# Second mixer: index scores rectified in PSUM, rounds moved between the low parts, differential output scaled late, weights of the second tile ahead

## The chip, the cores and the metric

One NeuronCore of a Trainium2 chip runs the whole program in one launch. The metric is the device time of an execution in microseconds (us); the value of a kernel is the median of its runs. All times in this document are us unless marked otherwise.

## The reference, cut to what matters

256 tokens of width 1024 in float32 pass through two blocks of two layers each. The change touches only the mixer of the second block (`hybrid_layer`), which is run twice (layer 0 and layer 1):

```python
h = rms_norm_2(x, attn_norm); proj = h @ w_in            # 1024 x 5444
aq, ak, av, iq, ik, iw, bq, bk, bv, gates = split_cols(proj)
# heads are normed and rotated; then, for path A (8 heads of 64, in pairs):
dots  = einsum(iq, ik) * 64**-0.5                        # 4 index heads
score = sum_h iw[h] * relu(dots[h]);  score[not causal] = -inf
top 64 keys of each query by score                       # k_sel = 256 // 4
ya = softmax(q k * 64**-0.5 over those keys) @ v
# path B (4 differential pairs): p0, p1 are two causal softmaxes
yb = (p0 - lam * p1) @ v;  yb = rms_norm_2(yb, b_subln) * (1 - lam_init)
x = x + (g_a * (ya @ w_up_a) + g_b * (yb @ w_up_b)) @ w_out
x = x + swiglu of rms_norm_2(x)                          # FFN, hidden 2816
```

The first block (FFN, another mixer, FFN, twice, then a norm) runs ahead of it, and its last norm is folded into the first norm of layer 0 here.

## The kernel before, in words

**Products.** Every float32 product with weights is made of three matmuls of the fast float32 form: high part by high part, high by low, low by high (`three`). A weight unit is 128 x 2048 elements (`raw`, four slots). It is loaded by a DMA from the SyncE queue, ScalarE writes its high part (`split` in the scalar block, to `w_hi`, line 717), VectorE subtracts that from the unit to get the low part (`split` in the vector block, `w_lo`, line 1222), and TensorE waits for `units_split`. A slot is used again four units later. `win_split(n, j)` is the split of unit j of tile n.

**Projection.** The 5444 columns are 11 tiles (`WIN2`), each of two units and 16 steps; a step is three matmuls of 128 x 128 by up to 512 columns. `full_k` runs a tile: its steps are numbered 0 to 15 (8 j + 4 i + c: unit j, token half i), and after each step it calls a function of the tile (`beside_bk`, `beside_aq`, ...) which may put other work on TensorE between the steps. Tile 2 (bk), 3 (aq), 4 (bv), 5 (ak), 6 (av), 7 to 10 (gates). Two PSUM banks take a tile; ScalarE evacuates both halves (`evac_half`), for the gates VectorE does (`gate`). GpSimd rotates the heads of a tile (`rotate2`) and signals `rot_ready`.

**What lies beside.** `turn(k)` transposes rotated heads by the identity, and `item(k)` copies them out of PSUM (even on ScalarE, odd on VectorE). `index_scores(h0)` puts the raw scores of two index heads into banks 4 and 5; ScalarE rectifies and scales them into `xn` (`index_relu`, signal `idx_relu`); VectorE adds them up with their weights (`index_score`, signal `idx_used`). `best(1)` is a round that finds the 8 largest scores of each token and marks them (`V.max`, `V.match_replace`, lines 1741 and 1744); eight rounds give 64. Then the marks are made a mask, which `masked(k)` adds for pairs 4 to 7.

**A pair** (0 to 3 differential, 4 to 7 sparse) passes through `pair_qk` (TensorE, banks 4 and 5), `masked` (VectorE), `exps` (ScalarE), `probs` (VectorE), `pair_turn` (TensorE, banks 6 and 7), `probs_turned` (ScalarE and, from pair 4 on, VectorE too), `diff_pv` or `sparse_pv` (TensorE), and, for a differential pair, `diff_out` (ScalarE, bank 2 to `xn`). After the norm of path B, TensorE turns it into banks 6 and 7, `diff_hi` and `diff_lo` split it, and `pair_turn(7)` waits for `diff_lo`, since it uses the same banks.

**Order.** Each engine's order is written out by hand in its block: a call that waits holds everything after it on that engine. There is no planner.

Of the kernel before, what the change touches and what calls it, by code (L numbers as in the profile page):

```python
# [15 lines left out]
ALU = mybir.AluOpType  # L16
ACT = mybir.ActivationFunctionType
# [5 lines left out]
P = 128  # L23
# [6 lines left out]
DH = 64  # L30
# [25 lines left out]
P2_WIN = 0  # L56
# [52 lines left out]
def build(nc, I, out):  # L109
    L = DEPTH  # L110
    with ExitStack() as ctx:
# [295 lines left out]

        relu = xn[:, :, 0:384]
# [299 lines left out]
        def _(act):  # L708
# [281 lines left out]
            for l in range(L):  # L990
# [4 lines left out]
                if l == 0:  # L995
# [8 lines left out]
                    square(6, 0, junk, 2)  # L1004
                    square_scaled(0)
                    stage(B, GAIN_ATTN, PARTS[2:], first=2)
                    split(st, 2)
# [52 lines left out]
                def index_relu(h):  # L1060

                    act.wait_ge(idx_done, l * 4 + h + 1)
                    if h >= 2:
                        act.wait_ge(idx_used, l * 4 + h - 1)
                    nc.scalar.activation(relu[:, h % 2, :], ps[:, 4 + h % 2, 0:384], ACT.Relu, scale=DH ** -0.5)\
                        .then_inc(idx_relu, 1)
# [19 lines left out]
                def diff_out(k):  # L1086

                    act.wait_ge(pair_out, J + (k + 1))
                    nc.scalar.activation(xn[:, :, 512 + P * k:512 + P * k + P],
                                         ps[:, 2, 0:2 * P].rearrange("p (i d) -> p i d", i=2), ACT.Copy)\  # L1090
                        .then_inc(diff_evac, 1)
# [21 lines left out]
                split(st, 3)  # L1113
# [29 lines left out]
                item(4)  # L1143
                head_roots(3)
                win_split(6, 0)
                act.wait_ge(lam_sums, l + 1)
                nc.scalar.activation(lam[:, 0:2], lam[:, 0:2], ACT.Exp).then_inc(lam_exp, 1)
                evac_half(4, 0)
# [38 lines left out]
                exps(7)  # L1187
                split(st, P2_UP + 1)
                diff_hi()
# [22 lines left out]
        def _(dve):  # L1212
# [453 lines left out]
            for l in range(L):  # L1666
# [3 lines left out]
                if l == 0:  # L1670
                    stage(B, GAIN_ATTN, PARTS[2:], first=2)
                    split(st, 2)
                    two_norms(N)
                    split(st, 3)
# [52 lines left out]
                def index_score(h):  # L1727

                    dve.wait_ge(idx_relu, l * 4 + h + 1)
                    for i, (c, n) in enumerate(((0, P), (P, 2 * P))):  # L1730
                        V.scalar_tensor_tensor(score[:, c:c + n], relu[:, h % 2, c:c + n], iw[:, i, h:h + 1],  # L1731
# [28 lines left out]
                def probs(k):  # L1760
# [3 lines left out]
                    V.drain()  # L1764
                    for i, (c, n) in enumerate(((0, P), (P, 2 * P))):
                        p0, p1 = (pair_p[:, k % 2, e, c:c + n] for e in range(2))
                        f0, f1 = (pair_factor[:, k % 2, e, i:i + 1] for e in range(2))
                        if k < 4:
                            V.tensor_scalar(p1, p1, f1, lam[:, 2:3], ALU.mult, ALU.mult)
# [3 lines left out]
                    if k < 4:  # L1773
                        V.drain()
                        for i, (c, n) in enumerate(((0, P), (P, 2 * P))):
                            p0, p1 = (pair_p[:, k % 2, e, c:c + n] for e in range(2))
# [972 lines left out]
```

## Time and profile before

| | |
|---|---|
| median of 3 runs | 1790.29 us (1788.45 to 1790.33) |
| the profiled execution | 1788.07 us, span of its instructions 1786.4 us |
| granted TensorE clock | 1.00 in every slice |
| busy: TensorE, VectorE, ScalarE, GpSimd | 99%, 69%, 55%, 13% of the span |
| second mixer, layer 0 | about 1020.9 to 1190 us |
| second mixer, layer 1 | about 1400 to 1570 us |

A timeline row is: start from the beginning of the span, duration, engine, line of the kernel, operation, output<-inputs by the program's names, shapes, count; in brackets idle time ahead of it and what ended it. Matmuls overlap: the next starts long before the drawn end of the one before. A `windows` row is: stretch, its length, then busy us and number of instructions of TensorE's matmuls, its weight loads, VectorE, ScalarE and GpSimd, then the granted clock, the DMA share and GB/s. Names: PE is TensorE, DVE VectorE, ACT ScalarE, POOL GpSimd.

### The profile page before, as it was taken

How to read it: one execution, taken by the hardware profiler on the slowest of the kernel's cores; microseconds unless marked ns; L12 is line 12 of the kernel's file. 1: busy time of each engine (PE TensorE's matmuls, PEld its weight loads, DVE VectorE, ACT ScalarE, POOL GpSimd, SP SyncE). 2: the span in 40 equal slices, each digit the busy share in tenths (PEclk: the TensorE clock that was granted, in tenths of full speed). 3: DMA queues.
4: the chain of work that ended last, by engine and by line, in shares of the span. 5: the costliest groups of instructions: out<-in, count | busy, mean ns of one | idle time of the engine just before them, and what ended most of it. 6: DMA issues, size and time to landing. Idle time of an engine off the chain costs nothing.

```text
span 1786.4 us, 25450 instructions
## 1 busy us (share of the span) xinstructions
PE 1773.3 (99%) x9448; PEld 1479.0 (83%) x9448; DVE 1231.7 (69%) x1753; ACT 988.0 (55%) x1333; POOL 226.2 (13%) x255
## 2 busy tenths in 40 slices
PE   9999999999999999999999999999999999999999
PEld 8888877888888888877888877778888877788887
DVE  6775667677557755767776489976775599867763
ACT  6554586565445554666555476555554466645551
POOL 0000131000000000320000096200001383100000
PEclk9999999999999999999999999999999999999999
DMA  8756472555546564544665563535656544545651
GB/s 266 221 195 203 138 211 73 188 188 188 212 145 195 194 224 143 190 119 143 195 197 198 166 212 124 181 128 182 201 195 207 168 162 143 188 159 173 192 202 75
DMA packets 221517, 316.26 MB, mean 177 GB/s; under 512 B 14168, under 2 KB 162288, under 8 KB 221168
## 3 DMA queue, kind: packets, MB, share of 16 engines
q1 hardware_dynamic: 221392, 315.02, 54.1%
q8 instruction: 57, 0.93, 0.2%
q14 instruction: 36, 0.29, 0.0%
q10 hardware_dynamic: 32, 0.01, 0.0%
HBM read 313.94 MB, written 1.05 MB: 176 GB/s over the span
## 4 chain that ended last, share of the span: by engine, by line
PE 84%; DVE 9%; DVEq 3%; ACT 2%; issue 1%; ACTq 0%; POOL 0%; POOLq 0%
PE ps L2091 25%; PE ps L1955 14%; PE ps L1957 13%; PE ps L1956 13%; PE ps L2092 13%; DVE w_lo L1222 3%; PE ps L1965 1%; ACT w_hi L717 1%; PE ps L2206 1%; PE ps L2179 1%; DVEq L1706 1%; PE ps L2194 1%; DVEq L1742 1%; DVE score L1731 1%; DVE att L1755 1%
## 5 line engine op out<-in xcount | busy, mean ns | idle before, releaser
L1222 DVE TENSOR_TENSOR w_lo<-raw,w_hi 128x2048 fp32r<-128x2048 f32 (+2 forms) x296 | 674.5, 2301 | 200.9 <-ACT w_hi L717 199.2
L2091 PE MATMUL ps<-aT,w_hi 128*128 128x512 f32 x1920 | 667.9, 392 | 0.0
L717 ACT ACTIVATE w_hi<-raw 128x2048 fp32r<-128x2048 f32 (+2 forms) x296 | 551.5, 1891 | 158.9 <-PE ps L1957 155.7
L2092 PE MATMUL ps<-aT,w_lo 128*128 128x256 f32 x1920 | 537.7, 280 | 0.0
L2091 PEld LDWEIGHTS ps<-aT,w_hi 128*128 128x128 f32 x1920 | 359.2, 187 | 79.8 <-issue 0.3
L2092 PEld LDWEIGHTS ps<-aT,w_lo 128*128 128x128 f32 x1920 | 362.9, 189 | 0.2
L1955 PE MATMUL ps<-w_hi,aT 128*128 128x512 f32 (+2 forms) x768 | 309.3, 403 | 4.3 <-DVE w_lo L1222 2.8
L1957 PE MATMUL ps<-w_hi,aT 128*128 128x512 f32 (+2 forms) x768 | 295.1, 384 | 0.0
L1956 PE MATMUL ps<-w_lo,aT 128*128 128x512 f32 (+2 forms) x768 | 294.2, 383 | 0.0
L1955 PE MATMUL ps<-w_hi,gT_hi 128*128 128x512 f32 x528 | 206.0, 390 | 0.0
L1957 PE MATMUL ps<-w_hi,gT_lo 128*128 128x512 f32 x528 | 205.6, 389 | 0.0
L1956 PE MATMUL ps<-w_lo,gT_hi 128*128 128x512 f32 x528 | 205.5, 389 | 0.0
L1955 PEld LDWEIGHTS ps<-w_hi,aT 128*128 128x128 f32 x768 | 144.3, 188 | 46.1 <-issue 16.6
L1957 PEld LDWEIGHTS ps<-w_hi,aT 128*128 128x128 f32 x768 | 144.1, 188 | 29.2
L1956 PEld LDWEIGHTS ps<-w_lo,aT 128*128 128x128 f32 x768 | 144.6, 188 | 22.9
L766 ACT ACTIVATE att<-ps 128x512 f32<-128x512 f32 x60 | 35.9, 599 | 162.6 <-PE ps L2092 162.5
L1957 PEld LDWEIGHTS ps<-w_hi,gT_lo 128*128 128x128 f32 x528 | 99.1, 188 | 20.8
L1955 PEld LDWEIGHTS ps<-w_hi,gT_hi 128*128 128x128 f32 x528 | 99.1, 188 | 20.5
L1956 PEld LDWEIGHTS ps<-w_lo,gT_hi 128*128 128x128 f32 x528 | 99.1, 188 | 20.2
L1313 DVE TENSOR_TENSOR att<-ps,att 128x512 f32<-128x512 f32 x60 | 41.5, 692 | 78.6 <-ACT att L771 78.6
L768 ACT ACTIVATE att<-att 128x512 f32<-128x512 f32 x60 | 37.9, 632 | 103.8 <-DVE att L1311 103.8
L618 POOL COPY tt<-proj 128x512 f32<-128x512 f32 x4 | 4.1, 1052 | 634.3 <-DVE proj L1453 634.3
(289 smaller groups left out, 1704.0 us busy)
## 6 DMA issues: line engine op xcount, KB each, us to landing
raw<-in_w_in SPq DMA_DIRECT2D x120, 512.0 KB, 4.6
raw<-in_w_ffn_down SPq DMA_DIRECT2D x88, 512.0 KB, 4.4
raw<-in_w_ffn_in SPq DMA_DIRECT2D x88, 512.0 KB, 5.0
raw<-in_w_ffn_gate SPq DMA_DIRECT2D x86, 512.0 KB, 4.1
raw<-in_w_ffn_up SPq DMA_DIRECT2D x86, 512.0 KB, 5.1
raw<-in_w_ffn_out SPq DMA_DIRECT2D x44, 512.0 KB, 4.7
raw<-in_w_out SPq DMA_DIRECT2D x32, 512.0 KB, 4.7
raw<-in_w_ck SPq DMA_DIRECT2D x8, 512.0 KB, 3.9
```

The source lines that it names most:

```text
L717: nc.scalar.activation(dst, src, ACT.Copy).then_inc(units_hi, 1)
L766: nc.scalar.activation(sil[:, b % 2], ps[:, bg:bg + 2, SEQ:2 * SEQ], ACT.Copy).then_inc(gate_lo, 1)
L768: nc.scalar.activation(sil[:, b % 2], sil[:, b % 2], ACT.Silu).then_inc(silu_done, 1)
L1222: V.tensor_tensor(o, a, h, ALU.subtract).then_inc(units_split, 1)
L1313: V.tensor_tensor(gg[:, b % 2], ps[:, bu:bu + 2, 0:SEQ], gg[:, b % 2], ALU.add)
L1706: V.drain()
L1731: V.scalar_tensor_tensor(score[:, c:c + n], relu[:, h % 2, c:c + n], iw[:, i, h:h + 1], (causal if h == 0 else score)[:, c:c + n], ALU.mul ...
L1955: M(o, ah, wh, start=start, stop=False)
L1956: M(o, ah, wl, start=False, stop=False)
L1957: return M(o, al, wh, start=False, stop=stop)
L2091: M(o, wh, aT[:, :, k, :], start=k == 0, stop=False, skip_group_check=True)
L2092: r = M(o[:, 0], wl, aT_hi[:, k, :], start=False, stop=k == KC - 1, skip_group_check=True)
```

## The change

In the mixer of the second block:

- `index_relu` rectifies in place, in PSUM; `index_score` reads the bank. So `index_scores(2)` and `pair_qk(0)`, which write these banks again, wait for VectorE's `idx_used` where they waited for ScalarE's `idx_relu`, and ScalarE no longer waits for a free half of `relu`.
- The places on TensorE move: the first turn from after step 8 to after step 11 of tile bk, the first index scores from 14 to 15, the second ones from step 2 to step 8 of tile aq, the second turn from 9 to 11.
- For a differential pair VectorE forms lam x s0 / s1 (s the sums of the exponentials), adds p1 times this to the unscaled p0 in one operation for each half, and `diff_out` on ScalarE applies 1 / s0, in two operations.
- Rounds: before 1 after split(5, 0), 1 after probs(1), 2 after head_scales(4), 2 after masked(3), 2 after gate(7, 0). Now 1 ahead of split(5, 0), 1 behind it, 1 after head_sums(3), 1 ahead of probs(0), 1 ahead of masked(1), 1 after probs(1), 1 after head_scales(4), 1 after masked(3). The mask is made ahead of split 16 of the projection, and gate(7, 0) comes behind masked(4).
- ScalarE: item(4) comes behind evac_half(4, 0), head_roots(3) and the exponential of lam.
- `diff_hi` and `diff_lo` come ahead of the split of unit P2_UP + 1 (on VectorE gate(10, 0) too).
- Layer 0 only: units 2 and 3 (the second tile's weights) are split ahead of the squares of the folded norm and its roots.

```diff
-                    square_scaled(0)
-                    stage(B, GAIN_ATTN, PARTS[2:], first=2)
                     split(st, 2)
+                    stage(B, GAIN_ATTN, PARTS[2:], first=2)
+                    split(st, 3)
+                    square_scaled(0)
...
                     act.wait_ge(idx_done, l * 4 + h + 1)
-                    if h >= 2:
-                        act.wait_ge(idx_used, l * 4 + h - 1)
-                    nc.scalar.activation(relu[:, h % 2, :], ps[:, 4 + h % 2, 0:384], ACT.Relu, scale=DH ** -0.5)\
-                        .then_inc(idx_relu, 1)
+                    bank = ps[:, 4 + h % 2, 0:384]
+                    nc.scalar.activation(bank, bank, ACT.Relu, scale=DH ** -0.5).then_inc(idx_relu, 1)
...
-                    nc.scalar.activation(xn[:, :, 512 + P * k:512 + P * k + P],
-                                         ps[:, 2, 0:2 * P].rearrange("p (i d) -> p i d", i=2), ACT.Copy)\
-                        .then_inc(diff_evac, 1)
+                    for i in range(2):
+                        o = nc.scalar.activation(xn[:, i, 512 + P * k:512 + P * k + P], ps[:, 2, P * i:P * i + P],
+                                                 ACT.Copy, scale=pair_factor[:, k % 2, 0, i:i + 1])
+                    o.then_inc(diff_evac, 1)
...
-                item(4)
+                win_split(6, 0)
+                evac_half(4, 0)
                 head_roots(3)
-                win_split(6, 0)
                 act.wait_ge(lam_sums, l + 1)
                 nc.scalar.activation(lam[:, 0:2], lam[:, 0:2], ACT.Exp).then_inc(lam_exp, 1)
-                evac_half(4, 0)
+                item(4)
...
                 exps(7)
+                diff_hi()
                 split(st, P2_UP + 1)
-                diff_hi()
...
                     split(st, 2)
+                    split(st, 3)
                     two_norms(N)
-                    split(st, 3)
...
-                        V.scalar_tensor_tensor(score[:, c:c + n], relu[:, h % 2, c:c + n], iw[:, i, h:h + 1],
+                        V.scalar_tensor_tensor(score[:, c:c + n], ps[:, 4 + h % 2, c:c + n], iw[:, i, h:h + 1],
...
+                    if k < 4:
+                        f1 = pair_factor[:, k % 2, 1, :]
+                        V.scalar_tensor_tensor(f1, f1, lam[:, 2:3], pair_sums[:, k % 2, 0, :], ALU.mult, ALU.mult)
+                        V.drain()
...
-                            V.tensor_scalar(p1, p1, f1, lam[:, 2:3], ALU.mult, ALU.mult)
+                            o = V.scalar_tensor_tensor(p0, p1, f1, p0, ALU.mult, ALU.add)
...
-                    if k < 4:
-                        V.drain()
-                        for i, (c, n) in enumerate(((0, P), (P, 2 * P))):
-                            p0, p1 = (pair_p[:, k % 2, e, c:c + n] for e in range(2))
-                            o = V.scalar_tensor_tensor(p0, p0, pair_factor[:, k % 2, 0, i:i + 1], p1, ALU.mult, ALU.add)
...
                 item(3)
+                best(1)
                 win_split(5, 0)
                 best(1)
+                win_split(5, 1)
                 head_sums(3)
+                best(1)
                 item(5)
-                win_split(5, 1)
                 masked(0)
...
+                best(1)
                 probs(0)
                 win_split(6, 0)
+                best(1)
                 masked(1)
...
-                best(2)
+                best(1)
                 split(st, P2_WIN + 15)
                 masked(3)
-                best(2)
+                best(1)
                 probs(3)
                 item(9)
-                split(st, P2_WIN + 16)
-                dve.wait_ge(bias_loaded, (l + 1) * 16)
-                dve.wait_ge(rot_ready, l * 5 + (4 * L + 5))
-                gate(7, 0)
-                best(2)
...
+                split(st, P2_WIN + 16)
                 masked(4)
+                dve.wait_ge(bias_loaded, (l + 1) * 16)
+                dve.wait_ge(rot_ready, l * 5 + (4 * L + 5))
+                gate(7, 0)
                 split(st, P2_WIN + 17)
...
                 probs(7)
-                split(st, P2_UP + 1)
                 diff_lo()
                 gate(10, 0)
+                split(st, P2_UP + 1)
                 split(st, P2_UP + 2)
...
                 def beside_bk(at):
-                    if at == 8:
+                    if at == 11:
                         rotated(0)
                         turn((0, 1))
-                    if at == 14:
+                    if at == 15:
...
                 def beside_aq(at):
-                    if at == 2:
-                        pe.wait_ge(idx_relu, l * 4 + 2)
+                    if at == 8:
+                        pe.wait_ge(idx_used, l * 4 + 2)
                         index_scores(2)
-                    if at == 9:
+                    if at == 11:
...
-                        pe.wait_ge(idx_relu, l * 4 + 4)
+                        pe.wait_ge(idx_used, l * 4 + 4)
                         pair_qk(0)
```

## Rows read from the trace of the kernel before

**Rows 1.** The page, busy time of each engine.
```profile
PE 1773.3 (99%) x9448; PEld 1479.0 (83%) x9448; DVE 1231.7 (69%) x1753; ACT 988.0 (55%) x1333; POOL 226.2 (13%) x255
```

**Rows 2.** Busy time in the second mixer of layer 0 and of layer 1.
```profile
1020.90:1190.00 169.10, 165.16 (x840) 129.61 (x839) 143.87 (x257) 108.69 (x173) 84.88 (x73) 1.00 0.49 162
1400.00:1570.00 170.00, 166.83 (x849) 131.14 (x848) 143.62 (x259) 106.01 (x174) 77.06 (x53) 1.00 0.49 161
```

**Rows 3.** Timeline of TensorE, layer 0, third tile: start, duration, instruction.
```profile
1039.97 0.39 PE L1955 MATMUL ps<-w_hi,aT 128*128 128x512 f32 x1
...
1047.91 0.39 PE L1957 MATMUL ps<-w_hi,aT 128*128 128x512 f32 x1
```

**Rows 4.** Timeline of TensorE, layer 0: starts that are late, idle in brackets.
```profile
1029.22 0.31 PE L1957 MATMUL ps<-w_hi,aT 128*128 128x324 f32 x1
1029.94 0.50 PE L1955 MATMUL ps<-w_hi,aT 128*128 128x512 f32 x1 [0.41 <-DVE w_lo L1222]
...
1036.44 0.50 PE L1955 MATMUL ps<-w_hi,aT 128*128 128x512 f32 x1 [0.72 <-DVE w_lo L1222]
...
1083.89 0.50 PE L1955 MATMUL ps<-w_hi,aT 128*128 128x512 f32 x1 [0.29 <-ACT proj L1031]
...
1089.25 0.39 PE L1957 MATMUL ps<-w_hi,aT 128*128 128x512 f32 x1
1089.78 0.55 PE L2505 MATMUL ps<-ident,att 128*128 128x128 f32 x3
...
1131.28 0.50 PE L1955 MATMUL ps<-w_hi,aT 128*128 128x512 f32 x1 [0.86 <-DVE w_lo L1222]
...
1167.68 0.84 PE L2505 MATMUL ps<-ident,att 128*128 128x128 f32 x6 [0.88 <-DVE yb_lo L1796]
```

**Rows 5.** Timeline of TensorE, layer 0: first turn, index scores, first pair, last pair.
```profile
1048.13 0.66 PE L2137 MATMUL ps<-ident,proj 128*128 128x128 f32 x4
...
1056.88 0.93 PE L2477 MATMUL ps<-tt 64*128 64x128 f32 x8
...
1080.38 0.93 PE L2490 MATMUL ps<-tt 64*128 64x128 f32 x8
...
1171.24 0.87 PE L2532 MATMUL ps<-xn,proj 128*64 128x256 f32 x8
```

**Rows 6.** Timeline of VectorE, layer 0.
```profile
1052.40 3.19 DVE L1222 TENSOR_TENSOR w_lo<-raw,w_hi 128x2048 fp32r<-128x2048 f32 x1 [0.17 <-ACT w_hi L717]
...
1055.68 3.22 DVE L1222 TENSOR_TENSOR w_lo<-raw,w_hi 128x2048 fp32r<-128x2048 f32 x1
...
1060.73 2.11 DVE L1731 SCALAR_TENSOR_TENSOR score<-xn,iw,score 128x128 f32<-128x128 f32 x2
...
1079.61 0.68 DVE L1355 TENSOR_SCALAR tt<-ps 128x512 f32<-128x512 f32 x1
...
1083.38 0.41 DVE L1755 CUSTOM_DVE_ANT_0 att<-ps,causal 128x256 f32<-128x256 f32 x1
...
1095.65 0.67 DVE L1769 TENSOR_SCALAR att<-att,factor,lam 128x128 f32<-128x128 f32 x2
...
1115.20 0.61 DVE L1741 MAX8 m<-score 128x8 f32<-128x128 f32 x2
...
1116.71 0.62 DVE L1741 MAX8 m<-score 128x8 f32<-128x128 f32 x2
...
1128.93 2.29 DVE L1222 TENSOR_TENSOR w_lo<-raw,w_hi 128x2048 fp32r<-128x2048 f32 x1
...
1167.45 0.74 DVE L1703 SCALAR_TENSOR_TENSOR proj<-ps,rstd,proj 128x512 f32<-128x512 f32 x1
...
1170.50 0.55 DVE L1785 COPY xn<-ps 128x384 f32<-128x384 f32 x1
```

**Rows 7.** Timeline of GpSimd, layer 0, fourth rotation.
```profile
1081.04 3.35 POOL L656 TENSOR_TENSOR proj<-proj,rg 128x512 f32<-128x512 f32 x1
```

**Rows 8.** Timeline of ScalarE, layer 0, before the exponential of lam.
```profile
1081.76 1.28 ACT L1147 ACT_TABLE_LOAD   x1
```

More of the change, by code:

```diff
@@ L406, in build @@
         HEAD_NORMS = ((0, 1792, 64, 2), (1, 1860, 32, 3), (2, 2372, 48, 4), (3, 0, 0, 0), (5, 512, 16, 1))
-        relu = xn[:, :, 0:384]
         h1 = tt1[0:60, 14:16, :].rearrange("p a n -> p (a n)").rearrange("p (k n) -> p k n", k=2)
@@ L1004, in _ @@
                     square(6, 0, junk, 2)
+                    split(st, 2)
+                    stage(B, GAIN_ATTN, PARTS[2:], first=2)
+                    split(st, 3)
                     square_scaled(0)
-                    stage(B, GAIN_ATTN, PARTS[2:], first=2)
-                    split(st, 2)
                     square(6, 1, junk, 2)
@@ L1112, in _ @@
                 evac(0)
-                split(st, 3)
+                if l > 0:
+                    split(st, 3)
                 head_squares(0)
@@ L1672, in _ @@
                     split(st, 2)
+                    split(st, 3)
                     two_norms(N)
-                    split(st, 3)
                 else:
```

## The prediction

> **What bounds the kernel now.** I read the page first. TensorE (PE) is busy in 99% of a span of 1786.4 us [rows 1]. That share says little, since matmuls overlap: one of 512 columns is shown as 0.39 us long, but from the start at 1039.97 to that at 1047.91 there are 35 of them, so the pitch is 7.94 / 35 = 0.227 us [rows 3]. A step of a projection tile is three matmuls, 0.68 us. PE is the bound while its starts keep this pitch, and all that the change can win is the time by which a start is later. So the second view is PE's timeline through the second mixer, about 1021 to 1190 us for layer 0 and 1400 to 1570 for layer 1. VectorE (DVE) is busy for 143.9 of 169.1 us in the first stretch and 143.6 of 170.0 in the second, so its queue, not ScalarE's (108.7), is the one that can be late for PE [rows 2].
>
> I price a stall as the distance between two starts less the usual one. Where the view prints an idle time, it counts from the drawn end, so 0.39 - 0.227 = 0.16 is added. Layer 0 has, by [rows 4]: on w_lo at 1029.94, 0.72 behind a matmul of 324 columns at 1029.22 whose own pitch I estimate at 324 / 512 x 0.227 = 0.14, so 0.58; 0.72 + 0.16 = 0.88 on w_lo at 1036.44; 0.29 + 0.16 = 0.45 on ScalarE's evacuation at 1083.89; 0.86 + 0.16 = 1.02 on w_lo at 1131.28; 0.88 + 0.16 = 1.04 on yb_lo at 1167.68. Where a turn by identity follows a matmul without a wait, its distance is 1048.13 - 1047.91, the pitch; at 1089.78 it is 0.53, a stall of 0.30. Of such small stalls there are five in each layer, between 0.06 and 0.38, together about 1.1. Layer 1 repeats the pattern, except for the first two, which belong to layer 0's start. The whole prize is thus 1.46 + 2 x (0.45 + 1.02 + 1.04 + 1.1) = 8.7 us, 0.49% of the span. No edit can be worth more.
>
> **Layer 0's second tile (units 2 and 3).** The splits of both units now come on ScalarE before the squares of the final norm, and on DVE before two_norms. ScalarE can start unit 2 right behind the first square, and DVE's two splits (2.29 each where nothing else runs, as at 1128.93 [rows 6]) then follow the staging directly: both stalls, 0.58 + 0.88 = 1.46, should go. The price is that the norm, and with it the first tile's evacuation, is later by an estimated 1.5 to 2 us (one split more ahead of it). What depends on that is GpSimd's (POOL's) first rotation. PE used it at 1048.13 [rows 5]; that job moves three steps back (8 to 11), which gives 2.04 us. Taken as hidden; if the cover is gone, it costs up to 1.
>
> **Rectified scores in PSUM.** The index score read xn, iw and score from SBUF: 2.11 for a head's two operations (at 1060.73) [rows 6], four heads per layer. A DVE operation with two tensors in SBUF waits for a POOL operation that runs, and the other way round: w_lo at 1055.68 takes 3.22 in place of 2.29, and POOL's product at 1081.04 takes 3.35 [rows 6, 7]. An operation with one tensor in PSUM doesn't: the masked scores at 1083.38 take 0.41 while that product is in flight. The new score is of this kind; by this row I take 0.7 for a head (0.28 + 0.41 for its 128 and 256 columns; between 0.6 and 0.8), so DVE gains 1.4 a head, 5.6 a layer. The ScalarE part writes PSUM where it wrote SBUF, with the same 384 columns; I put it at no change.
>
> The Trainium skill (VectorE: DVE Perf Modes, section on the TRN2 errata) gives a fixed part of 120 cycles for a PSUM source and 58 for an SBUF one, which speaks against this edit: 65 ns for each of the 16 operations. The row of 0.41 for 256 columns agrees with the higher figure (0.39). By the page the gain would be 5.1 a layer where I take 5.6; PE's time would move by no more than that difference at one wait.
>
> But the edit adds a wait. PE may write banks 4 and 5 again only when DVE has read them: index_scores(2) and pair_qk(0) now wait for idx_used. PE's side: the old place is 1056.88 [rows 5], six steps earlier than the new one, so 1060.9. DVE's side: the first turn moves three steps back, to 1050.2, and with it the chain item(0), head squares, split (3,1), which began 4.27 behind the turn (1052.40 against 1048.13) [rows 5, 6]: now 1054.4. Then come two splits, 2.3 each free or 3.2 each beside POOL, and two heads of 0.7: 1060.4 to 1062.2. POOL rotates in all of this stretch, so I take 1061.8: **a new stall of 0.9 in each layer, bounds 0 and 1.4**. Behind it on PE's queue is everything.
>
> **Rounds moved ahead.** A round is 1.51 (1115.20 to 1116.71) [rows 6]. Eight remain. Before, one lay ahead of item(5); now three do, and split (5,1) too. DVE up to item(5): -5.6 (scores) + 3.0 (two rounds) + 2.3 to 3.2 (split) + 2.0 (the turn that starts the chain is later, and DVE waits for it) = 1.7 to 2.6 later than 1079.61 + 0.68 [rows 6]. That is 1082.0 to 1082.9. PE wants pair_qk(0), which waits for item(5), at 1080.32 + 0.9 = 1081.2 [rows 5]. ScalarE's item(4) now stands behind head_roots(3) and the exponential's table (1.28) [rows 8] and so comes about 2.4 behind head_sums(3), the same as DVE's round and item(5). POOL's third rotation meets three splits instead of two, which can hold turn((4, 5)) by the same amount. **New stall here: 1.3 in each layer, bounds 0 (no collisions) and 2.8 (each of three splits and a small operation waits 1.3 for POOL).** In return evac_half(4, 0) comes ahead of the roots and the table: 0.45 gone.
>
> What the early rounds buy lies at 1131.28: split(17) stood behind the last two rounds, the final mask and masked(4). With six rounds done before and masked(4) bound by pair_qk(4) alone, it ends some 3 us before it is wanted. 1.02 gone, and the following small stalls too: I take the 1.1 of them whole.
>
> **Differential output.** Two tensor_scalar for each of four pairs go (0.67 for both without POOL, at 1095.65) [rows 6], one tiny product and its drain come (about 0.2): 0.5 or more per pair off DVE, 2 a layer, most of it in stretches in which DVE then waits for PE. ScalarE gets a second operation of 128 columns, about 0.3, four times, beside idle time. Nothing on PE.
>
> **diff_hi and diff_lo ahead of P2_UP + 1.** The stall of 1.04 goes: diff_lo no longer waits behind a split of 2.3. But gate(10, 0) now stands ahead of both splits, and it can't begin before step 11 of the last tile has ended, 0.68 before the unstalled turn: 1167.68 - 1.04 - 0.68 = 1165.96, with the tail of the pipe 1166.1. Then gate 0.74, two splits 2.2 each, the copy of probs_turned(7) 0.55 (rows at 1167.45, 1128.93 and 1170.50) [rows 6]: 1171.8, and PE a little behind it. sparse_pv(7) needs this copy and ran at 1171.24 [rows 5]. PE thus gets there 0.7 later than now, not 1.0 earlier: **-0.7 in each layer**; bounds +1.0 (the copy is in time after all) and -1.2.
>
> **Sum.** Gains 1.46 + 2 x (0.45 + 1.02 + 1.1) = 6.6; new waits 2 x (0.9 + 1.3 + 0.7) = 5.8. Left: 0.8 us faster. The profiled execution took 1788.07 (span 1786.4 and 1.7 around it), 2.2 below the median of 1790.29; I subtract from the median: 1789.5.
>
> **Rivals.** (1) The new waits don't bite: if DVE's splits fall between POOL's operations, idx_used comes at 1060.4, item(5) before 1081, and only the tail is lost. 6.6 - 1.4 = 5.2 faster, 1785.1; with the tail won as well, 8.7, 1781.6. For it: DVE gains 5.6 a layer where it was never idle. Against it: the chain starts 2 us later and POOL is busy throughout. (2) Slower, by one mechanism: VectorE's queue ahead of item(5) and head_sums(3). Three rounds and both splits of tile 5 stand there, and if the splits each wait for POOL, pair_qk(0) stalls 2.8 and the index wait 1.4, in both layers: 2 x (1.4 + 2.8 + 0.7) - 6.6 = 3.2 slower, 1793.5; with the tail at its bound of -1.2 it is 4.2, 1794.5, past the 3.6 that can be told from no change. It decides from the point where this queue ends over 2 us behind 1081.2. The Trainium skill (SBUF - State Buffer, section SBUF: two separate sides) says that the shared port pair is held for a whole instruction and the other side blocks entirely; by that rule, the trace agrees, each collision costs a whole POOL operation and this rival is possible. (3) The edits to idle stretches do nothing: stalls merely move between places, and the time stays within 1 us. It is my forecast by another road.
>
> **Chances.** Forecast with (3), within 3.6 us of before: 0.60. Rival 1: 0.28. Rival 2 or more: 0.12. A change under 0.2% (3.6 us) is about what a measurement of this kernel can't tell from none. The range goes from 1785.4, near rival 1, to 1793.0, short of rival 2: faster 0.28, same 0.60, slower 0.12.
>
> **What would show it.** Right: no PE idle at the second tile of layer 0, at tile 5's second half and at 1131; index scores near 0.7 a head with no lengthening beside POOL; PE waiting before index_scores(2) by about 1, before turn((4, 5)) or pair_qk(0) by about 1.3, and before sparse_pv(7) by about 1.7, where nothing waited. Wrong: any of these three waits missing, or a fourth at masked(1) and probs(1), which now stand behind two more rounds.

## The result, and the profile after

The changed kernel takes 1791.65 us (median of 22 runs, 1789.49 to 1793.52), the kernel before 1788.45 on the same chips (22 runs); the medians are 3.2 apart. The ratio of the means is 1.0015, 95% interval 1.0008 to 1.0021, without one execution of the kernel before that took 6164.18 us. So the changed kernel is slower by 2.7 us (1.4 to 3.8), where 0.8 faster was forecast. The profiled execution took 1791.19, its span is 1789.5.

The page of the changed kernel, busy time of each engine, and then its `windows` rows of the two stretches of the second mixer:

```profile
PE 1772.6 (99%) x9448; PEld 1480.1 (83%) x9448; DVE 1213.3 (68%) x1745; ACT 990.4 (55%) x1341; POOL 224.8 (13%) x255
```
```profile
1020.90:1190.00 169.10, 163.61 (x839) 130.05 (x838) 136.28 (x258) 110.40 (x180) 83.14 (x73) 1.00 0.48 162
1400.00:1570.00 170.00, 164.54 (x845) 130.64 (x845) 132.89 (x255) 107.01 (x177) 77.59 (x53) 1.00 0.49 162
```

These are the same clock times as in [rows 2], but this execution reaches the second mixer 1.9 us later in both layers (its first matmul starts at 1022.90 where the kernel before has 1020.99), for a reason that lies in the first block and not in the change (last section). So times of two profiles are compared from the same TensorE instruction on. In stretches moved by as much (1022.8 to 1191.9 and 1401.93 to 1573.1) VectorE has 8.6 and 10.1 us less work than before, as the edit to the scores and to the differential output promised, and the part of the stretch in which TensorE is not busy grows from 3.9 and 3.2 us to 5.5 and 5.5: it waits more. TensorE's waits (line, what it waited for, total, times, longest):

```profile
PE ps L2533 <- DVE xn L1783: 3.8, 2, 1.9
PE ps L2138 <- POOLq L664: 2.8, 2, 1.4
PE ps L2478 <- DVEq L1733: 2.6, 2, 1.3
PE ps L2146 <- POOLq L577: 1.7, 1, 1.7
PE ps L1956 <- ACT proj L1030: 1.4, 2, 0.7
```

Four of them come twice, once in each layer, and all four are new. Their places in layer 0, from TensorE's timeline:

```profile
1062.53 0.93 PE L2478 MATMUL ps<-tt 64*128 64x128 f32 x8 [1.31 <-DVEq L1733]
...
1080.29 1.09 PE L2138 MATMUL ps<-ident,proj 128*128 128x128 f32 x8 [1.40 <-POOLq L664]
...
1100.75 0.50 PE L1956 MATMUL ps<-w_hi,aT 128*128 128x512 f32 x1 [0.68 <-ACT proj L1030]
...
1173.18 0.87 PE L2533 MATMUL ps<-xn,proj 128*64 128x256 f32 x8 [1.89 <-DVE xn L1783]
```

These are index_scores(2), turn((4, 5)), the step after step 3 of tile av, and sparse_pv(7). The views print the idle time from the drawn end of a matmul; a time called "as drawn" below is this one. Priced like the stalls of before (distance of starts less the usual one, so some 0.1 to 0.2 more) they are 1.37, 1.55, 0.85 and 1.96 in layer 0, and 1.38, 1.52, 0.85 and 1.96 in layer 1. The stalls of [rows 4] are all gone. Counted that way, layer 0 had 5.05 of stalls and has 5.73, layer 1 had 4.23 and has 5.87 (with 0.16 at its second tile). Between the same TensorE instructions of the two executions, layer 0 takes as long as before (to 0.02) and layer 1 1.19 more; distances of about 0.1 us, which I don't count as stalls, make up the difference.

That is 1.2 of the 2.7. The two profiled executions are 3.1 us apart; the other 1.9 lies in the first block, where the code is the same. So the remaining 1.5 of the 2.7 can't be read from these two traces. The granted clock of a whole execution was 1.0 in 5 of the 22 runs of the changed kernel (median 1790.0) and 0.998 or 0.999 in the other 17 (median 1792.0); the experiments below show a fall of this clock behind long waits, and what it costs.

### The profile page after: what moved, and what is told of

Same layout as the page of the kernel before. It is cut to its first block, busy times and chain, and to the rows that moved or that the text cites. A ratio compares the mean times of both kernels' runs of the same rounds, so it can differ in the third digit from the quotient of the medians.

```text
span 1789.5 us, 25446 instructions
## 1 busy us (share of the span) xinstructions
PE 1772.6 (99%) x9448; PEld 1480.1 (83%) x9448; DVE 1213.3 (68%) x1745; ACT 990.4 (55%) x1341; POOL 224.8 (13%) x255
## 4 chain that ended last, share of the span: by engine, by line
PE 87%; POOL 4%; issue 2%; DVE 2%; POOLq 2%; ACT 1%; DMA 1%; SPq 0%; DVEq 0%; ACTq 0%
PE ps L2092 25%; PE ps L1956 14%; PE ps L1958 14%; PE ps L1957 14%; PE ps L2093 13%; PE ps L1966 1%; PE ps L2207 1%; PE ps L2180 1%; POOL rg L672 1%; POOL proj L656 1%; DVE w_lo L1221 1%; PE ps L2195 1%; PE ps L2138 1%; POOL proj L647 1%; PE ps L2491 1%
```

## The experiments

Edits are shown against the changed kernel, unless said otherwise. The kernel before ran beside every group, with medians of 1788.59 (first four), 1788.09 (next four), 1789.85 (comb_a to comb_c) and 1788.53 (last).

**The end of the mixer on VectorE (e1_tail).**

```diff
                 diff_lo()
-                gate(10, 0)
                 split(st, P2_UP + 1)
-                split(st, P2_UP + 2)
                 probs_turned(7)
+                gate(10, 0)
+                split(st, P2_UP + 2)
                 gate(10, 1)
```

> Edit to the changed kernel: VectorE's order at the end of the mixer is diff_lo, split of P2_UP + 1, probs_turned(7), gate(10, 0), split of P2_UP + 2, in place of diff_lo, gate(10, 0), both splits, probs_turned(7). Theory (sparse_pv(7) waits for VectorE's copy, which the order put behind gate(10, 0) and two splits): PE's wait of 1.96 us before sparse_pv(7) goes in both layers and nothing takes its place, 3.9 us less than the changed kernel, about 1787.5 where that one has 1791.4. Rival (the copy waits for the last pair's turn, or a split of the up-projection becomes late instead): less than 1 us is won.

Measured: 1786.05 (1785.17 to 1788.01, 10 runs), ratio to before 0.9984 (0.9975 to 0.9994). In the trace the wait before sparse_pv(7) is gone and nothing took its place: 2.0 less between the same TensorE instructions of each layer. But the median fell by 5.6, not 3.9, and all ten executions had a clock of 1.0. VectorE's timeline at this place, first of the changed kernel, then of this one:

```profile
1165.36 1.29 DVE L1794 TENSOR_TENSOR yb_lo<-ps,yb_hi 128x512 fp32r<-128x512 f32 x2 [2.64 <-ACT yb_hi L1102]
1167.22 0.75 DVE L1702 SCALAR_TENSOR_TENSOR proj<-ps,rstd,proj 128x512 f32<-128x512 f32 x1 [0.57 <-PE ps L1958]
1168.07 4.49 DVE L1221 TENSOR_TENSOR w_lo<-raw,w_hi 128x2048 fp32r<-128x2048 f32 x2
1172.48 0.55 DVE L1783 COPY xn<-ps 128x384 f32<-128x384 f32 x1
```
```profile
1166.69 2.29 DVE L1221 TENSOR_TENSOR w_lo<-raw,w_hi 128x2048 fp32r<-128x2048 f32 x1 [1.00 <-ACT w_hi L715]
1168.90 0.55 DVE L1783 COPY xn<-ps 128x384 f32<-128x384 f32 x1
1169.37 0.74 DVE L1702 SCALAR_TENSOR_TENSOR proj<-ps,rstd,proj 128x512 f32<-128x512 f32 x1
```

The copy that TensorE needs stood behind 5.2 us of work (gate(10, 0) and both splits) that nobody wanted yet; with one split ahead of it, it isn't waited for.

**The split beside the third rotation (e2_split51).**

```diff
-                win_split(5, 1)
                 head_sums(3)
                 best(1)
                 item(5)
+                win_split(5, 1)
                 masked(0)
```

> Edit to the changed kernel: the low part of unit (5, 1) goes back behind item(5) on VectorE, the rounds stay. Theory (turn((4, 5)) waits for GpSimd's third rotation, and that is late because a third split of 2048 columns lies beside it, each holding it for 1.9 us): rotation 2 takes 14 us in place of 15.8, the wait of 1.55 us before turn((4, 5)) goes in both layers, 3.1 us less than the changed kernel. Rival (the three rounds ahead of item(5) do it, or GpSimd's later start alone): the wait stays at 1 us or more and the time within 1 us of the changed kernel.

Measured: 1793.0 (8 runs), ratio to before 1.0021 (1.001 to 1.0031). The wait before turn((4, 5)) is gone, and the third rotation takes 13.89 us (1062.57 to 1076.46), where in the changed kernel it took 15.77 (1064.42 to 1080.19) and in the kernel before 14.21. This split and GpSimd's last two products beside it, in the changed kernel:

```profile
1075.16 3.12 DVE L1221 TENSOR_TENSOR w_lo<-raw,w_hi 128x2048 fp32r<-128x2048 f32 x1
```
```profile
1076.28 3.91 POOL L663 TENSOR_TENSOR proj<-proj,ms 128x512 f32<-128x512 f32 x2
```

So the split made it, not the three rounds, which still stand there. But nothing was won: TensorE's waits of this kernel show the same time a little later,

```profile
PE ps L1956 <- ACT proj L1030: 3.9, 2, 2.0
PE ps L2533 <- DVE xn L1783: 3.8, 2, 1.9
PE ps L2478 <- DVEq L1733: 2.6, 2, 1.3
```

since ScalarE's evacuation in tile av is bound by its own chain and TensorE reached it 1.5 earlier. Both theories failed on the time: one price went, the next rose by 1.3 (0.68 to 1.98 as drawn). And the clock fell twice in this execution, in layer 1 within 1 us of that wait (0.97 in the window 1440 to 1500) and in layer 0 behind the wait before sparse_pv(7); all eight runs had a clock of 0.997 to 0.999.

**Scores through SBUF (e3_sbuf).** `relu` in `xn`, `idx_relu` and `idx_used` are as in the kernel before.

```diff
+                    if h >= 2:
+                        act.wait_ge(idx_used, l * 4 + h - 1)
+                    nc.scalar.activation(relu[:, h % 2, :], ps[:, 4 + h % 2, 0:384], ACT.Relu, scale=DH ** -0.5)
...
-                        V.scalar_tensor_tensor(score[:, c:c + n], ps[:, 4 + h % 2, c:c + n], iw[:, i, h:h + 1],
+                        V.scalar_tensor_tensor(score[:, c:c + n], relu[:, h % 2, c:c + n], iw[:, i, h:h + 1],
...
-                        pe.wait_ge(idx_used, l * 4 + 2)
+                        pe.wait_ge(idx_relu, l * 4 + 2)
```

> Edit to the changed kernel: the rectified index scores go to SBUF again and VectorE reads them there, PE waits for idx_relu as before; all else as changed. Theory of the prediction (a score from SBUF costs VectorE 1.4 us a head more and PE's wait before index_scores(2) comes from the scores in PSUM alone): that wait of 1.37 goes, but item(5) and the third rotation come 2 to 5 us later, so PE waits 3 to 6 us before turn((4, 5)) or pair_qk(0): 3 to 8 us slower than the changed kernel in all. Rival (VectorE has slack there): 2.7 us faster than the changed kernel.

Measured: 1805.1 (4 runs), 13.4 slower than the changed kernel: the direction of the theory, and more than its 3 to 8. All four runs had a clock of 0.994, so falls of the clock are in this number too. The wait before index_scores(2) is gone, as said; the two waits before pair_qk(0) make 14.7. ScalarE's row shows the road:

```profile
1085.06 0.22 ACT L1056 ACTIVATE ms<-ms 128x16 f32<-128x16 f32 x1 [9.21 <-DVE ms L1719]
```

head_roots(3) waits 9.21 for VectorE's head_sums(3), behind the scores, two splits and two rounds, and item(4) stands behind it. With the scores in SBUF this order, with its early rounds, doesn't pay. VectorE's scores in this kernel, and below them those of the changed kernel:

```profile
1061.18 2.11 DVE L1734 SCALAR_TENSOR_TENSOR score<-xn,iw,score 128x128 f32<-128x128 f32 x2
...
1067.87 2.81 DVE L1734 SCALAR_TENSOR_TENSOR score<-xn,iw,score 128x128 f32<-128x128 f32 x2
```
```profile
1061.70 0.74 DVE L1730 SCALAR_TENSOR_TENSOR score<-ps,iw,score 128x128 f32<-128x128 f32 x2
...
1066.39 0.73 DVE L1730 SCALAR_TENSOR_TENSOR score<-ps,iw,score 128x128 f32<-128x128 f32 x2
```

**The first turn at its old place (e4_turn8).**

```diff
                 def beside_bk(at):
-                    if at == 11:
+                    if at == 8:
                         rotated(0)
                         turn((0, 1))
-                    if at == 15:
+                    if at == 14:
```

> Edit to the changed kernel: first turn after step 8 and first index scores after step 14 of tile bk, as before; the rest stays. Theory (the waits before index_scores(2) and turn((4, 5)) come from the chain that starts with this turn): in layer 1 both go or fall below 0.5 us, 2.5 us gained. In layer 0 GpSimd's first rotation ends later than before because units 2 and 3 are split ahead of the norm, so PE waits 1.7 us at the turn itself, and gains as much of the two later waits. Total about 2.5 us less than the changed kernel. Rival (the place of the turn has nothing to do with them): nothing in layer 1, 1.7 us lost in layer 0.

Measured: 1789.18 (10 runs), ratio to before 1.0006 (0.9997 to 1.0016): by the medians 2.5 less than the changed kernel, as expected. The trace supports less: 0.3 in each layer, with a fall of the clock in layer 1 (about 1.6, see e12), so some 2.2 without it. The wait before index_scores(2) is gone in both layers, that before turn((4, 5)) fell only to 0.9 as drawn in both, where under 0.5 was expected in layer 1, and layer 0 has one of 1.3 at the first turn. So the wait before index_scores(2) comes from the chain that this turn starts, the other one only in part.

The chain reaches GpSimd too, through its third product of the second rotation, which waits for ScalarE's head squares. Layer 1 of the changed kernel, and below it of this one:

```profile
1435.09 1.29 POOL L653 TENSOR_TENSOR proj<-proj,rg 128x512 f32<-128x512 f32 x1 [1.92 <-ACT proj L1041]
```
```profile
1431.51 1.30 POOL L653 TENSOR_TENSOR proj<-proj,rg 128x512 f32<-128x512 f32 x1
```

In layer 0 that wait is 0.38. The second rotation itself begins no later than before, counted from the mixer's first matmul (27.06 us behind it against 27.22 in layer 0, 28.66 against 28.65 in layer 1).

**The index scores two steps later (e5_idx10).** `if at == 8` is `if at == 10` in `beside_aq`.

> Edit to the changed kernel: index_scores(2) two steps later on PE, after step 10 of tile aq in place of 8. Theory (the wait before turn((4, 5)) is set by GpSimd's queue, not by PE's): the wait of 1.37 us before index_scores(2) goes in both layers, but PE then comes 1.4 us earlier to turn((4, 5)) and waits there 2.9 us in place of 1.55; nothing is won as long as the clock holds, and where it falls behind so long a wait, 1.5 us or more is lost. Rival (two separate prices): 2.7 us less than the changed kernel.

Measured once, 1793.76; this execution has the slower pace of the first block (last section), as the profiled one of the changed kernel has, which took 1791.19. The wait before index_scores(2) is gone, that before turn((4, 5)) is 2.7 in place of 1.5. TensorE's timeline in layer 1:

```profile
1461.17 0.39 PE L1958 MATMUL ps<-w_hi,aT 128*128 128x512 f32 x1
1464.11 1.93 PE L2138 MATMUL ps<-ident,proj 128*128 128x128 f32 x8 [2.55 <-POOLq L664]
1465.69 0.78 PE L1956 MATMUL ps<-w_hi,aT 128*128 128x512 f32 x1
1466.27 0.63 PE L1957 MATMUL ps<-w_lo,aT 128*128 128x512 f32 x1
1466.70 0.63 PE L1958 MATMUL ps<-w_hi,aT 128*128 128x512 f32 x1
```

A wait ahead of another on one engine hides a part of it; 1.37 and 1.55 don't add up as prices. And behind the longer wait the starts are 0.43 apart in place of 0.227: the lower of the clock's two levels. The clock fell a second time in this execution, in layer 0 behind the wait before sparse_pv(7).

**One round later (e6_round_late).**

```diff
                 win_split(6, 0)
-                best(1)
                 masked(1)
...
                 head_scales(4)
-                best(1)
+                best(2)
```

> Edit to the changed kernel: the round ahead of masked(1) goes behind head_scales(4). Theory (the wait of 0.85 us after step 3 of tile av is ScalarE's evacuation of tile ak, which stands behind exps(1), and this waits for masked(1) behind the round of 1.5 us): it goes in both layers, 1.7 us less than the changed kernel, and no other wait appears. Rival (ScalarE's own queue sets it): it stays above 0.5 us.

Measured once, 1788.08. The wait in tile av is gone from the list of waits, the other three are unchanged; layer 0 took 0.7 and layer 1 0.6 less than in the changed kernel. The theory holds for the cause; the gain is 1.3 where 1.7 was expected.

**GpSimd's rotations left out (e7_no_rotation).**

```diff
+                    if q > 0:
+                        pool.wait_ge(head_scale, l * 5 + q + 1)
+                        nc.gpsimd.drain()
+                        pool.sem_inc(rot_ready, 1)
+                        continue
                     rotate2(c0, w,
```

> Edit to the changed kernel, to measure what GpSimd's work beside VectorE costs: GpSimd leaves out the rotation and scaling of all heads but those of tile 1 (HEAD_NORMS 1 to 4) in the second block and only signals, so the heads of the outputs are unrotated. Theory (VectorE's two-tensor operations in SBUF and GpSimd's hold each other up, and this sets both waits): every w_lo of this stretch takes 2.3 us in place of up to 3.2, the waits before index_scores(2) and turn((4, 5)) go or fall below 0.3 us, those of av (0.85) and sparse_pv(7) (1.96) stay or change by less than 0.5; the index scores stay at 0.73 a head. Rival (VectorE's order alone sets the wait before index_scores(2)): that wait stays above 1 us.

Measured once, 1784.13. Every low part between 1054 and 1075 takes 2.23 to 2.29. The waits before index_scores(2) and turn((4, 5)) are gone, that before sparse_pv(7) is the same 1.9; in tile av 0.17 is left, less than the theory had. VectorE's order is unchanged, so the rival fell: the wait before index_scores(2) isn't there unless the two engines hold each other up. For turn((4, 5)) this run shows less, since GpSimd's rotation, for which TensorE waits there, is itself left out; for that wait e2 and e11_comb_c are the tests. The Trainium skill (SBUF - State Buffer, SBUF: two separate sides) says that VectorE and GpSimd share a pair of ports, which one instruction holds for its whole length while the other engine blocks; the trace agrees, with 3.1 to 3.2 for a low part beside GpSimd and 2.3 without.

**The second tile's weights alone (e8_early_tile), against the kernel before.** The same lines as in the change: both splits of units 2 and 3 ahead of the norm.

> Edit to the kernel before: units 2 and 3 of layer 0 are split ahead of the final norm's squares, as in the change, and nothing else. Theory: both stalls at the second tile's weights (0.58 and 0.88 us) go. The first rotation is 1.5 to 2 us later, and the first turn, here still after step 8, waits for it by about 1.3 us. Net 0 to 0.5 us less than before. Rival (the later rotation is hidden): 1.5 us less.

Measured: 1787.96 (10 runs), ratio 0.9998 (0.9989 to 1.0008). Both stalls are gone and layer 0 is 0.28 faster: the first turn, still after step 8, waits 1.4 as drawn for GpSimd. GpSimd's first rotation begins 2.0 later (1033.89 against 1031.91) but ends no later (the second begins at 1047.94 against 1048.21); the turn waits because TensorE comes to it 1.7 earlier. The edit pays its 1.5 only with a later turn, and the later turn is what delays the chain.

**The edits together (e9_comb_a, e10_comb_b, e11_comb_c).** e10_comb_b is the changed kernel with the tail of e1, the split of e2, two rounds later, and these places:

```diff
-                best(1)
                 probs(0)
                 win_split(6, 0)
-                best(1)
                 masked(1)
...
                 head_scales(4)
-                best(1)
+                best(2)
                 split(st, P2_WIN + 15)
                 masked(3)
-                best(1)
+                best(2)
...
-                    if at == 11:
+                    if at == (10 if l == 0 else 8):
                         rotated(0)
                         turn((0, 1))
-                    if at == 15:
+                    if at == (15 if l == 0 else 14):
...
-                    if at == 8:
+                    if at == (9 if l == 0 else 8):
                         pe.wait_ge(idx_used, l * 4 + 2)
```

e9_comb_a leaves the turns where the change put them and has the second index scores after step 10; e11_comb_c is comb_b with the split (5, 1) where the change put it.

> Four edits together to the changed kernel: low part of (5, 1) behind item(5); both rounds between item(5) and masked(1) moved behind head_scales(4) and masked(3); index_scores(2) after step 10; tail order diff_lo, split, probs_turned(7), gate(10, 0), split. Theory: the waits before index_scores(2) (1.37) and sparse_pv(7) (1.96) go, that before turn((4, 5)) falls from 2.9 (as it is without the first) to 1.0, that in tile av goes or stays below 0.7 since all before it is earlier. Per layer 1.37 + 0.55 + 0.5 + 1.96 = 4.4 less than the changed kernel, and no fall of the clock: about 1781 where the changed kernel's median is 1791.7 and the kernel before's 1788.1. Rival (the waits move to the next place, as in the run with only the first edit): 1784 or more.

> As comb_a, but the chain is started earlier: first turn after step 10 in layer 0 and 8 in layer 1 of tile bk, first index scores after 15 and 14, second ones after step 9 and 8 of tile aq. Theory: no wait at any of the four places above 0.5 us, 5 us a layer less than the changed kernel, about 1780. Rival (the wait in tile av is now as long as all that was won before it): 0.9 us a layer more than that.

> As comb_b, but the low part of (5, 1) ahead of head_sums(3) as in the changed kernel. Theory (this split beside the third rotation costs GpSimd 1.5 to 1.9 us): the wait before turn((4, 5)) is 0.9 us in each layer, the kernel 1 to 2 us slower than comb_b. Rival (with the earlier turn it is hidden): the same as comb_b.

Measured: comb_a 1781.01, ratio 0.995 (0.9933 to 0.9966); comb_b 1779.3, ratio 0.9942 (0.9925 to 0.9958); comb_c 1782.31, ratio 0.9955 (0.9938 to 0.9972), four runs each. The first two came within 0.7 of their numbers; comb_c lost 3.0 where 1 to 2 was expected. Both layers together take 9.1 us less in comb_b than in the kernel before. TensorE's waits of comb_b in the whole program:

```profile
PE ps L2144 <- POOLq L577: 1.7, 1, 1.7
PE ps L1954 <- DVE w_lo L1408: 0.5, 1, 0.5
PE ps L1964 <- DVE x L1275: 0.4, 2, 0.2
PE ps L2136 <- POOLq L664: 0.2, 1, 0.2
```

The first stands before the program's first matmul and the second within its first 15 us. The two of 0.2 lie at the start of the two second mixers and are the same in the kernel before; of the waits that the change is about only the last is left. In comb_c the wait before turn((4, 5)) is 3.0 as drawn for the two layers, 2.1 of it in layer 0, and the clock fell behind that one; GpSimd's last two products of the third rotation, first in comb_c, then in e2_split51, where they begin at the same time but without the split beside them:

```profile
1074.41 3.91 POOL L663 TENSOR_TENSOR proj<-proj,ms 128x512 f32<-128x512 f32 x2
```
```profile
1074.41 2.05 POOL L663 TENSOR_TENSOR proj<-proj,ms 128x512 f32<-128x512 f32 x2
```

**One wait alone and the clock (e12_comb_b_tail_old).** comb_b with VectorE's tail as in the changed kernel.

> As comb_b, but the end of the mixer in the changed kernel's order (gate(10, 0) and both splits ahead of probs_turned(7)), so that one wait of 1.96 us before sparse_pv(7) in each layer is the only one left. Theory (such a wait costs more than its length, since the granted clock falls to half behind it in a part of the executions): 3.9 us for the two waits plus up to 1.7 for each fall, about 1784 to 1786 where comb_b has 1779.3, with mean clocks of 0.998 or 0.999 in most executions where comb_b has 1.0. Rival (the wait costs its length alone, the lower clocks of the changed kernel come from its other waits): 1783.2 and clocks of 1.0.

Measured: 1783.2 (five runs). Three have a clock of 1.0 and 1782.93, 1783.11 and 1783.2, which is comb_b and 3.9; two have 0.999 and 1784.41 and 1784.45, 1.35 more. So both had a part: the median is the rival's number, and most of these executions paid the two waits' length alone, where the theory had a fall in most; two paid more. The profiled one shows both sides, with the same wait before L2531 in both layers (1.89 as drawn). Windows around it, layer 0 and layer 1, the clock third from the end, and layer 0's timeline:

```profile
1160.00:1180.00 20.00, 18.11 (x82) 14.28 (x80) 13.91 (x12) 14.23 (x11) 0.00 (x0) 0.91 0.46 158
1540.00:1562.00 22.00, 20.11 (x97) 16.05 (x96) 16.80 (x16) 14.28 (x11) 0.00 (x0) 1.00 0.49 166
```
```profile
1168.39 1.20 PE L2531 MATMUL ps<-xn,proj 128*64 128x256 f32 x8 [1.89 <-DVE xn L1783]
1169.52 0.80 PE L1954 MATMUL ps<-w_hi,yb_hi 128*128 128x512 f32 x1
1170.11 0.63 PE L1955 MATMUL ps<-w_lo,yb_hi 128*128 128x512 f32 x1
1170.54 0.63 PE L1956 MATMUL ps<-w_hi,yb_lo 128*128 128x512 f32 x1
...
1172.24 0.40 PE L1954 MATMUL ps<-w_hi,yb_hi 128*128 128x512 f32 x1
1172.47 0.39 PE L1955 MATMUL ps<-w_lo,yb_hi 128*128 128x512 f32 x1
```

From 1170.11 on six starts are 0.43 apart, then 0.23 again. Between the same TensorE instructions layer 0 takes 3.55 more than in comb_b and layer 1, with the same wait and no fall, 1.96: by the trace this fall cost 1.6.

## Why the prediction was wrong

The step that failed is the sum of the new waits. Counted like the stalls, the prediction had 2 x (0.9 + 1.3 + 1.7) = 7.9 us of them (the 1.7 before sparse_pv(7) stands in its sum as the 1.04 not won and 0.7 lost), and 11.4 were measured: all three were larger than forecast, and a fourth of 0.85 in each layer had no term. Beside it a wait was priced at its length, and the clock can fall behind it. Term by term:

- **Second tile**: right. 1.46 forecast, 1.63 won in layer 0. That the cover was the later turn is shown by e8. The price was thought to be a first rotation that is 1.5 to 2 later; it begins 2.1 later and ends no later, and the cover is needed because TensorE comes earlier.
- **Scores in PSUM**: right. 0.73 a head beside GpSimd, against 0.7. The wait that it adds was mis-sized: 1.37 in place of 0.9, just inside the bound of 1.4. Counted from the first turn, TensorE wanted the banks 10.7 us behind it, as in the sum; the second head ended 12.0 behind it where the sum had 11.6. The sum counted GpSimd's hold on the large splits, and not on the 16-column product of head_sums, 1.30 in place of 0.34.
- **Wait at turn((4, 5)) or pair_qk(0)**: 1.3 forecast, 1.55 and 1.52 measured, at the first. The size was near, the reason half wrong. The forecast put VectorE's queue ahead of item(5), with its rounds, first; e2 shows that it is GpSimd's queue. Its third rotation is 1.6 longer than before in layer 0 and 1.2 in layer 1, by the third split beside it, and in layer 1 it begins 1.5 later, since the second one waits 1.92 for the chain of the later turn. In layer 0 it begins no later, but TensorE has lost 1.6 less at the second tile. VectorE then waited 2.18 us for TensorE before masked(0), so item(5) decided nothing.
- **Rounds ahead**: the gain at split(17) and the small stalls came as forecast. What failed is the price of nothing for masked(1) behind a round: VectorE reached it late, exps(1) and with it ScalarE's evacuation followed, and TensorE waited 0.85 in each layer. Taking the round away won 1.3 of these 1.7 (e6). The prediction named this wait as a sign of being wrong, and it stands in no sum.
- **Tail**: 0.7 a layer lost forecast; 0.92 and 0.67 measured (1.04 and 1.29 won, 1.96 lost).
- **The price of a wait**: the other step that failed. Each was priced at its length. In e12 a fall of the clock behind a wait of 1.96 cost 1.35 more by the times and 1.6 by the trace. The profiled execution of the changed kernel has no such fall, so a sum made against a profile misses it. e1 took the longest wait away: 3.9 by the trace and 5.6 by the medians, with all clocks back at 1.0.
- **The whole prize**: 8.7 was called the most that any edit can be worth. The stalls of before that the change took away add up to 9.1 (layer 1 has 4.1 of them where the sum has 3.6), and comb_b won 9.1 in the two layers.

Together: 0.8 faster as forecast, 11.4 - 7.9 = 3.5 more of waits, and 9.1 - 8.7 = 0.4 more of stalls that went, make 2.3 slower. The trace has 1.2; the other 1.1 lies in distances of about 0.1 us, which neither sum counts. What the times have beyond the trace, 1.5 of the 2.7, stays partly open. If each of the 17 runs with a lower clock had one fall, it is 17 / 22 x 1.35 to 1.6 = 1.0 to 1.2; that is worked out, not shown run by run. Against it stands that the kernel before had a clock of 0.999 in 9 of its 51 runs beside the experiments, and that the share of runs in the slower pace of the first block, which costs 1.9, isn't known for either kernel.

The absolute time was forecast from 1790.29, a median of three runs of which two lie near 1790.3; with 22 runs the kernel before has 1788.45. The forecast of 1789.5 thus has a base that is 1.8 too high, and only the difference says how good it was. By the difference rival 2 (3.2 slower) came nearest, and its wait before index_scores(2), 1.4, is the measured one. Its reason was not: it had 2.8 at pair_qk(0) from VectorE's queue, where nothing waited, and left out the fourth wait and the clock. That its total fits is in part luck. Of the two gains that the prediction names for the scores, 5.6 and 5.1 a layer, the rows are nearer to the first: the second head takes 0.74 in place of 2.11, which for four heads makes 5.5.

## What to carry to other kernels

When edits give an engine slack and spend it at once, ask for each thing moved ahead who stands behind it, also two engines further on: the fourth wait runs from a round on VectorE over exps(1) on ScalarE to TensorE. A wait moved ahead of another hides it, so prices on one engine are to be tested together: no single edit to the waits in the middle of the mixer took out what the combination did. A long wait should be broken up before several short ones, since it can cost the clock besides. And times of two profiles are compared from the same instruction on, since what lies ahead of it may have taken a different time.

## What the runs showed of the hardware

**Behind a wait of about 2 us the granted clock may fall, and that cost 1.35 to 1.6 us more.** In the profiled executions of e2, e4, e5, comb_c and e12 TensorE had run at full pace, then stood for 1.9 to 2.6 us as drawn, and within 1 us ran three to seven starts at 0.43 us for 512 columns (1.2 GHz) in place of 0.227 (2.4 GHz); in layer 1 of e2 narrower matmuls lay between. With the same wait twice in one execution (e12), the clock fell behind one and not behind the other, and in the profiled executions of the changed kernel, e6 and e7 it fell behind none of these. Leaving out the idle time before the program's first matmul, e1 has no wait above 1.4, e8 none above 1.4, comb_a none above 1.6 and comb_b none above 0.5, and all their 28 runs had a clock of 1.0. The kernel before has none above 1.1 either, and yet 9 of its 51 runs beside the experiments had 0.999. None of these was profiled, so what fell there is open, and long waits aren't shown to be the only cause. The Trainium skill (TensorE: Matmul & The Clock Gate, Part 1) says that a monitor of recent activity sets the clock, and that its windows run free of the program; two equal waits with unlike outcomes agree with that, and no run here shows more of it.

**The first block has two paces.** The runs of the kernel before lie mostly at 1787.8 to 1788.6 or at 1789.7 to 1790.7, and a few at 1792.4 to 1792.7. The profiled executions of the changed kernel, e5 and e7 take 1.7 to 1.9 us more than the others from their 50th to their 1,000th TensorE instruction, before anything that was changed, at a granted clock of 1.00. That the upper runs of the kernel before are of this kind fits, but none of them was profiled. A pair of matmuls (512 and 256 columns) starts every 0.353 us there (changed kernel) against 0.346 (comb_b):

```profile
72.72 0.40 PE L2092 MATMUL ps<-aT,w_hi 128*128 128x512 f32 x1
...
75.90 0.40 PE L2092 MATMUL ps<-aT,w_hi 128*128 128x512 f32 x1
```
```profile
71.80 0.40 PE L2090 MATMUL ps<-aT,w_hi 128*128 128x512 f32 x1
...
73.53 0.39 PE L2090 MATMUL ps<-aT,w_hi 128*128 128x512 f32 x1
```

(9 pairs in 3.18, 5 pairs in 1.73.) Its cause stays open; it is the reason why profiles have to be compared from the second mixer's first matmul on.
